# Cached keys turned in 32 by 32 blocks on VectorE instead of 128 by 128 on TensorE, in a two-layer decoder step

## The reference, cut to what matters

```python
kbar = mean(kb, axis=2)                       # kb: heads, blocks of 256 keys, 128
g = einsum('hqd,hnd->hqn', qf, kbar)          # block score; top 3 past blocks are kept
s = einsum('hqd,hqnkd->hqnk', qf, ks) - slopes * dist
p = softmax(s)                                # over the kept blocks and the own one
out = einsum('hqnk,hqnkd->hqd', p, vs)
```

## Time and profile before

| | us |
|---|---|
| median of three executions | 1229.66 |
| profiled execution, its own time | 1224.0 |
| its span | 1222.3 |
| K stage: from the own-token scores (334.3) to the last score group's end (487.1) | 152.8 |
| V stage: from there to about 638 | 151 |

### The profile page before, as it was taken

The page is one execution under the profiler, slowest core; times in us unless marked ns, Lnnn a source line. Parts: engine busy times, 40 slices in busy tenths (PEclk is TensorE's granted clock), DMA queues, the critical chain, the costliest instruction groups (busy, mean ns, idle before and its releaser), DMA issues.

```text
span 1222.3 us, 23737 instructions
## 1 busy us (share of the span) xinstructions
PE 1176.9 (96%) x9352; PEld 1042.2 (85%) x9352; DVE 713.0 (58%) x1355; ACT 564.2 (46%) x714; POOL 331.5 (27%) x207
## 2 busy tenths in 40 slices
PE   5899999999999999999999999899999989999997
PEld 2589798878888787787788898899999889999997
DVE  3746555545544546633545447489999996583112
ACT  3333324333354444422333237576666656575443
POOL 1000000000000002200000002667666778605773
PEclk9999999999999999999999999999999999999998
DMA  9999899999898878899999997585848445454542
GB/s 332 339 331 343 283 334 314 375 354 355 290 313 305 277 259 295 258 371 328 338 372 342 321 331 200 174 280 165 283 156 275 138 142 184 140 174 156 166 145 94
DMA packets 236962, 324.87 MB, mean 266 GB/s; under 512 B 12429, under 2 KB 152525, under 8 KB 236429
## 3 DMA queue, kind: packets, MB, share of 16 engines
q1 hardware_dynamic: 233472, 312.78, 75.7%
q0 software_dynamic: 2192, 7.79, 2.2%
q10 hardware_dynamic: 1188, 2.79, 0.7%
HBM read 317.96 MB, written 7.06 MB: 266 GB/s over the span
## 4 chain that ended last, share of the span: by engine, by line
PE 76%; DVE 16%; DMA 3%; issue 2%; ACT 2%; SPq 1%; POOL 0%; DVEq 0%; ACTq 0%
PE PS L307 19%; PE PS L311 18%; PE PS L310 18%; DVE PS L1763 10%; PE PS L395 5%; PE PS L987 4%; DMA XR<-in_ada_w 3%; PE PS L1014 3%; PE PS L1245 2%; DVE WLO L301 1%; PE PS L410 1%; SPq L382 1%; PE PS L1971 1%; ACT WHI L296 1%; DVE PS L1757 0%
## 5 line engine op out<-in xcount | busy, mean ns | idle before, releaser
L307 PE MATMUL PS<-HH,WHI 128*128 128x288 f32 x2176 | 662.4, 304 | 16.7 <-DVE HL L1683 4.5
L311 PE MATMUL PS<-HH,WLO 128*128 128x288 f32 x2176 | 643.9, 296 | 0.0
L310 PE MATMUL PS<-HL,WHI 128*128 128x288 f32 x2176 | 643.7, 296 | 0.0
L307 PEld LDWEIGHTS PS<-HH,WHI 128*128 128x128 f32 x2176 | 410.9, 189 | 38.2 <-issue 32.0
L296 ACT ACTIVATE WHI<-WRAW 128x1024 fp32r<-128x1024 f32 x272 | 283.8, 1056 | 344.1 <-PE PS L311 291.2
L310 PEld LDWEIGHTS PS<-HL,WHI 128*128 128x128 f32 x2176 | 411.2, 189 | 0.0
L311 PEld LDWEIGHTS PS<-HH,WLO 128*128 128x128 f32 x2176 | 410.6, 189 | 0.0
L301 POOL TENSOR_TENSOR WLO<-WRAW,WHI 128x1024 fp32r<-128x1024 f32 x117 | 281.1, 2422 | 192.6 <-ACT WHI L296 192.6
L301 DVE TENSOR_TENSOR WLO<-WRAW,WHI 128x1024 fp32r<-128x1024 f32 x155 | 191.1, 1235 | 158.1 <-ACT WHI L296 157.9
L1763 DVE SCALAR_TENSOR_TENSOR PS<-ACTS,CWT,PS 128x288 f32<-128x288 f32 x448 | 192.5, 516 | 0.0
L1739 ACT ACTIVATE ACTS<-ACTS 128x1088 f32<-128x1088 f32 x32 | 70.4, 2200 | 59.8 <-DVE ACTS L1761 34.6
(11 more groups left out here) (280 smaller groups left out, 748.1 us busy)
## 6 DMA issues: line engine op xcount, KB each, us to landing
XR<-in_ada_w SPq DMA_DIRECT2D x192, 512.0 KB, 8.5
WRAW<-in_ab_w_in SPq DMA_DIRECT2D x112, 512.0 KB, 7.3
WRAW<-in_c_w_in SPq DMA_DIRECT2D x96, 512.0 KB, 3.6
XR<-in_cache_b_k SPq DMA_DIRECT2D x128, 256.0 KB, 5.2
XR<-in_cache_b_v SPq DMA_DIRECT2D x128, 256.0 KB, 5.5
WRAW<-in_ab_w_out SPq DMA_DIRECT2D x32, 512.0 KB, 8.9
WRAW<-in_c_w_out SPq DMA_DIRECT2D x32, 512.0 KB, 3.3
ACTS<-in_x_prompt ACTq DMA_DIRECT2D x2, 1024.0 KB, 11.1
```

Source lines behind the costliest of these rows:

```text
L307: first = pe.matmul(out, whi, HH[:, k, :], start=start, stop=False)
L310: pe.matmul(out, whi, HL[:, k, :], start=False, stop=False)
L311: return pe.matmul(out, wlo, HH[:, k, :], start=False, stop=stop)
```

## The change

- TensorE turns no keys. VectorE turns each slot of XR in four instructions of 128 by 512 (`k_turn`), one per head, into four tiles KT[0] to KT[3]. The instruction turns 32 by 32 blocks in place, so a key's 128 dimensions lie as four blocks of 32, with 32 tokens of each of the four token groups on the partitions.
- The queries are spread to fit (`q_spread` on TensorE, `q_fill` on ACT and VectorE, tile BD, zeroed by GpSimd): a row of the scores is now (sequence, token group, query), and each head has columns of its own. A score group (`k_scores`) is one head: 16 float32 matmuls over 64 columns instead of 8 over 256 for two heads; there are 8 per unit instead of 4. It stands half a unit behind: heads 0 to 3 in the second half of their unit, heads 4 to 7 in the first half of the next.
- A row of a query is spread over four partitions. Gates, maxima and sums are therefore folded across partitions on TensorE (`gate_sum`, `max_turn`, `max_back`, `z_sum`), the probabilities are scaled by ACT (`row_norm`), and `probs_turn` becomes, per b, 8 pieces of 16 matmuls and one of 4, 32 columns each, where 9 transposes were.
- The mean of the gating branch moves from unit 5 to unit 2, its centring to unit 3. Page numbers are read a unit ahead.

```diff
-        def k_turn(pe, u, c, g4):
-            g, hh, j2 = 16 * u + 4 * c + g4, 2 * (c // 2) + g4 // 2, g4 % 2
-            if g >= 2:
-                pe.wait_ge((kt_a, kt_d)[g % 2], g // 2)
-            for h2 in range(2):
-                for t in range(2):
-                    at = 512 * (2 * j2 + t) + P * ((2 * hh + h2) % 4)
-                    last = pe.transpose(PS[:, (M2, M3)[g % 2], (2 * h2 + t) * P:(2 * h2 + t + 1) * P],
-                                        XR[:, c, at:at + P], IDENT[:])
-            last.then_inc(kt_tr, 1)
+        def k_turn(dve, u, c):
+            half = c // 2
+            dve.wait_ge(x_rdy[c], need(17 + u, c))
+            for x in range(4):
+                if c % 2 == 0 and (u or half):
+                    dve.wait_ge(ks_head, 8 * u + 4 * half + x - 3)
+                dve.transpose(KT[x][:, 4 * (c % 2):4 * (c % 2) + 4, :],
+                              XR[:, c].rearrange("p (a n) -> p a n", a=4)[:, :, P * x:P * x + P]).then_inc(kt_tr, 1)
+            dve.wait_ge(kt_tr, 16 * u + 4 * c + 4)
+            dve.sem_inc(x_used[c], 1)
...
-        def k_scores(pe, u, hh):
-            for h2 in range(2):
-                h = 2 * hh + h2
-                for j in range(4):
-                    last = pe.matmul(PS[32 * j:32 * j + 32, M0, 0:BLOCK], QM[:, j, h, :], KT[:, hh % 2, j, h2, :],
-                                     start=h == 0, stop=h == HEADS - 1)
+        def k_scores(pe, u, h):
+            g, h2, bank = h // 2, h % 2, (M0, M2)[u % 2]
+            pe.wait_ge(kt_tr, 16 * u + 8 * (h // 4) + 4 + h % 4 + 1)
...
+            for e in range(4):
+                for j in range(4):
+                    x = (4 * e + j) * 4 + g
+                    last = pe.matmul(PS[32 * j:32 * j + 32, bank, 64 * g:64 * g + 64], BD[:, x, 16 * h2:16 * h2 + 32],
+                                     KT[h % 4][:, 2 * j:2 * j + 2, 32 * e:32 * e + 32],
+                                     start=h2 == 0 and e == 0, stop=h2 == 1 and e == 3)
...
             for u in range(8):
-                for c in range(4):
-                        k_turn(pe, u, c, g4)
-                        rest_part(pe, n, g, x_used[c] if g4 == 3 else None)
...
+                for s in range(16):
+                    rest_part(pe, 16 + 2 * u + s // 8, s % 8)
+                    if u == 0 and s < 4:
+                        q_spread(pe, 0, s)
+                    if s % 2 and u + s // 8:
+                        k_scores(pe, u if s > 8 else u - 1, s // 2 % 4 if s > 8 else 4 + s // 2)
+                    if u == 3 and 10 < s < 15:
+                        q_spread(pe, 1, s - 11)
...
+                    if u == 7 and 6 < s < 16:
+                        probs_turn(pe, 0, s - 7)
...
+            for h in range(4, HEADS):
+                k_scores(pe, 7, h)
...
             for u in range(8):
                 for c in range(4):
+                    if (u, c) == (0, 2):
+                        q_fill(dve, 0, (0, 1))
+                    if (u, c) == (4, 2):
+                        q_fill(dve, 1, (0, 1))
...
+                    if u and c == 2:
+                        scores_take(dve, u - 1)
+                    k_turn(dve, u, c)
                     if c % 2 == 0:
                         lo(dve, 67 + 2 * u + c // 2)
+                    if (u, c) == (5, 0):
+                        choose_blocks(dve, 0)
...
+            rows = IDENT[:].rearrange("p (x i q) -> p i x q", i=4, q=DS)
+            for g in range(4):
+                for i in range(4 if t < 8 else 1):
+                    dst = PS[32 * i:32 * i + 32, probs_bank(b, f), (t % 4) * P:(t % 4 + 1) * P]
+                    last = pe.matmul(dst.rearrange("p (j r) -> p j r", j=4)[:, :, 8 * g:8 * g + 8],
+                                     SROW[b][:, g, 32 * t:32 * t + 32], rows[:, i], start=True, stop=True)
```

More of the change, by code:

```diff
@@ new lines, in q_spread @@
+        def q_spread(pe, b, e):
+            if e == 0:
+                if b:
+                    pe.wait_ge(g_ln, 1)
+                else:
+                    pe.wait_ge(s_pc, HEADS)
+                    pe.wait_ge(s_pf, HEADS)
+            rhs = Q[:, :, SR0 + 16 * b:SR0 + 16 * b + 16].rearrange("p h (s i) -> p s h i", i=DS)
+            for i in range(4):
+                dst = PS[32 * i:32 * i + 32, M3, P * e:P * e + P].rearrange("p (s h i) -> p s h i", s=4, h=HEADS)
+                last = pe.matmul(dst, IDENT[:, 32 * e:32 * e + 32], rhs, start=True, stop=True)
+            last.then_inc(s_qr, 1)
@@ new lines, in q_fill @@
+        def q_fill(eng, b, tokens):
+            eng.wait_ge(s_qr, 4 * b + 4)
+            if b:
+                eng.wait_ge(ks_head, 32)
+            else:
+                eng.wait_ge(s_bdz, 1)
+            for i in tokens:
+                src = PS[32 * i:32 * i + 32, M3, :].rearrange("p (x h q) -> p x h q", h=2, q=DS)
+                for h2 in range(2):
+                    at = 32 * h2 + DS * i
+                    dst = BD[32 * i:32 * i + 32, :, at:at + DS]
+                    if tokens[0]:
+                        eng.activation(dst, src[:, :, h2, :], ACT.Copy).then_inc(s_bdf, 1)
+                    else:
+                        eng.tensor_copy(dst, src[:, :, h2, :]).then_inc(s_bdf, 1)
@@ L1016, in k_scores, with gate_sum @@
             last.then_inc(ks_head, 1)
-        def probs_turn(pe, b, f):
-            if f:
-                pe.wait_ge(s_ptc, 3 * b + f)
-            else:
-                pe.wait_ge(s_exp, b + 1)
-            for t in range(4 * f, min(9, 4 * f + 4)):
-                n = P if t < 8 else 32
-                last = pe.transpose(PS[0:n, M1, (t % 4) * P:(t % 4 + 1) * P], SROW[:, t * P:t * P + n], IDENT[:])
-            last.then_inc(s_ptt, 1)
+        def gate_sum(pe, b):
+            pe.wait_ge(ks_free, 4 * b + 4)
+            if b:
+                pe.wait_ge(s_ptc, 3)
+            pe.matmul(PS[:, M1, 0:16], SAME, GATE.rearrange("p h n -> p (h n)"), start=True, stop=True).then_inc(s_gs, 1)
@@ new lines, in max_turn, with max_back, z_sum, probs_bank @@
+        def max_turn(pe, b):
+            pe.wait_ge(s_rm, b + 1)
+            pe.transpose(PS[0:4, M1, 0:P], RMAX, IDENT[:]).then_inc(s_mt, 1)
+        def max_back(pe, b):
+            pe.wait_ge(s_mf, b + 1)
+            pe.transpose(PS[:, M1, 128:132], MROW, IDENT[0:4, 0:4]).then_inc(s_mb, 1)
+        def z_sum(pe, b):
+            pe.wait_ge(s_exp, 4 * b + 4)
+            pe.matmul(PS[:, M1, 0:4], SAME, ZSUM, start=True, stop=True).then_inc(s_zs, 1)
+        def probs_bank(b, f):
+            return M1 if f != 1 else (M3, M0)[b]
@@ L1110, in k_act @@
             for u in range(8):
-                for c in range(4):
-                    k_save(act, u, c, 0)
-                    if c % 2 == 0:
-                        hi(act, 67 + 2 * u + c // 2)
-                    k_save(act, u, c, 2)
-                    if u < 2 and c % 2:
-                        x = 2 * u + c // 2
+                if u == 0:
+                    q_fill(act, 0, (2, 3))
+                hi(act, 67 + 2 * u)
+                if u < 2:
+                    for x in (2 * u, 2 * u + 1):
@@ new lines, in k_act, with key_bias @@
+                if u in (2, 4, 6):
+                    silu_zt(act, 51 + u // 2, u // 2 - 1)
+                if u == 6:
+                    root(act, 2)
+                if u == 7:
+                    row_norm(act, 0)
+                hi(act, 68 + 2 * u)
+                if u == 6:
+                    row_exp(act, 0)
+            for f in range(3):
+                probs_save(act, 0, f)
+        def key_bias(dve):
+            dve.wait_ge(s_iota, 1)
+            for g in range(4):
+                dve.tensor_scalar(ALB[:, g, :], IOTA, TOKROW, SLOPE[:, g:g + 1], ALU.add, ALU.mult)
@@ L2135, in _ @@
                         load_ada(sp, 32, 16, c)
+                if half and v < 7:
+                    regs = page_numbers(sp, v + 1)
                 w_load(sp, 89 + 2 * k)
```

397 lines of the change are left out of this document (216 added, 181 removed).

## The result

The changed kernel takes 1264.2 us in the median (1262.5 to 1276.3, 4 runs) where the kernel before takes 1227.2: a ratio of 1.031, 95% interval 1.027 to 1.036. It is **slower**, by 37 us. I had forecast slower by 14.6, and the time is just outside the range.

The account below looks back on a forecast made before the run. TensorE's list of instructions was taken as the bound; K stage 9.3, V stage 5.1 and 0.2 more us sum to 14.6, giving 1244 us against the median, with an 8-in-10 range of 1217 to 1264.

Parts of the forecast that it names:

- loop wait: K stage: TensorE waits 1.9 us per half unit for VectorE's turn, low part and next turn, covered by two products.
- 3.2 on top of the wait: K stage, `q_fill` for b = 1: the next score group needs three more turns and four copies, 3.2 us extra.
- 2.1: K stage: `choose_blocks`, eleven small instructions on VectorE, adds 2.1 us to the irregular part.
- TensorE waits 1.9 us in every half unit. It is then 6.5 + 1.9 = 8.45 us: K stage: a half unit takes 8.45 us instead of 8.98, so of 39 us only 8.5 remain gained.
- My list without the clock: K stage: irregular items of 26.9 us plus sixteen halves, 135.2, gave 162 us instead of 152.8.
- The V stage: 5.1 forecast: V stage: b = 1 probabilities 5.2 us instead of 1.2, and folds 1.1, on a TensorE without gaps.
- rival 5: Short matmuls bound by their issue: a score group costs 1.2 us, 23 us more, 1267 us; chance 0.10.
- Dearer turns (4): Turns of two passes, 1.14 us each: VectorE binds, K stage 203 us, whole 1285 us; chance 0.07.
- cheaper groups (2): Switches between kinds cost nothing, a score group is 0.65 us, K stage 151, whole 1232 us; chance 0.12.
- No loop wait: Turns so fast that TensorE never stands; loads at 374 GB/s bind, half a unit 7.0 us, whole 1213; chance 0.14.
- No change from SP's page numbers: SP reads page numbers while it would wait; as DMA isn't the bound, this costs nothing.
- the right mechanism: The forecast case: the loop wait takes most of what leaves TensorE; own range 1234 to 1258 us, chance 0.57.

Follow-up runs that it names:

- experiments 5: Changed kernel with the second softmax's probability pieces spread over two weight chunks of the V stage, one per two products: 1265.7 us.
- experiment 6: Changed kernel with page numbers read at the start of their unit, as before the change: 1267.9 us.
- experiment 2: Changed kernel with 16 unread matmuls on TensorE ahead of the first score group of each half unit: 1255.0 us.
- 8 to 10: Changed kernel with GpSimd low parts, spread pieces, reordered VectorE items; then three low parts ahead of GpSimd's sums of squares; then unread matmuls: 1237.5, 1229.2, 1235.7 us.
- experiment 3: Changed kernel with VectorE turning both slots of a half unit head by head, the low part ahead: 1240.9 us.
- experiment 10: Combined kernel with earlier GpSimd low parts, plus 8 to 22 unread matmuls ahead of ten score groups: 1235.7 us.
- experiment 1: Changed kernel with the low part ahead of the four turns of an even slot, not behind them: 1242.2 us.
- experiment 4: Changed kernel with the 16 low parts of the K stage on GpSimd, not on VectorE: 1249.2 us.

## Why the prediction was right or wrong

**The direction and the mechanism were right.** TensorE lost its turns and got a loop wait in exchange. The terms, forecast and measured: product 0.40 and 0.40, score group 0.83 and 0.78, turn 0.60 to the next start and 0.59 (four in 2.48, the last 0.70), loop wait 1.9 and 1.84, piece of the probabilities 0.58 and 0.58. Of the irregular waits, the first score group's was 5.58 us, that at the refill of the queries 5.45, at the block choice 3.46; "3.2 on top of the wait" and "2.1" gave 5.1 and 4.0.

**What failed is the step "TensorE waits 1.9 us in every half unit. It is then 6.5 + 1.9 = 8.45 us"**: it prices a wait by its length. The regular half that kept its clock (from 359.35; one in each of the traces of experiments 5 and 6 as well), and those of experiment 2, lasted 8.19 to 8.21; the usual half lasted 9.66 to 9.68, because the clock was at 1.2 GHz for part of the work behind the wait. That is 1.5 us, on a term of 0.53 gained per half: the sign of a regular half turned, from 8.98 before to 9.66. My list without the clock gives 161 in the table's measure, and 176.8 was measured, 15.6 more. The clock accounts for more than that: 0.85 over the 177.7 us, between the levels 1.00 and 0.50, are 53 us at 1.2 GHz, and in the half from 367.5 (0.82 over 9.70) 3.5 such us cost 1.47. At that rate 53 us cost up to 22 (an estimate, too high by the part that fell on waits). So the rest of the list came out some 5 us too high and hid part of the miss: 64 score groups at 0.78 for 0.83 are 3.2 of it, 16 waits of 1.84 for 1.9 are 1.0. The row that could have warned me was the granted clock itself: 1.00 in stages without gaps, and I took it as given for a stage into which I was putting 16 gaps of 2 us.

**The V stage: 5.1 forecast, 10.4 measured.** The pieces cost what I said. Missing were the 2.24 us stop in the middle of a piece and the low clock behind it, which together are some 3.7 of the missing 5.3 us (2.24, and the 1.47 that such a stretch cost in the regular half: an estimate); the rest stays open. Without a stop or with short ones the V stage took 152.3 to 154.3 (experiments 5, 8 to 10), 5.5 to 7.5 above before. The stop is part of rival 5 (short matmuls bound by their issue), but as a stop after a dense stretch, not as a dearer record. The floor of about 25 ns from start to start that the Trainium skill, TensorE: Matmul & The Clock Gate, gives (section on 56 ns and 53.3 ns) didn't show here: a piece's 16 matmuls (32 records) and their loads ran in 0.46 us, and the trace has them starting 17 ns apart on the mean, in four column groups side by side.

**Rivals.** Dearer turns (4) and cheaper groups (2) are excluded by the rows above. "No loop wait" (3) was tried in experiment 3: with the regular waits removed the K stage was still 155 us, not 16 halves of 7.0, and loads aren't shown as its bound, with one wait for a page of 4.4 us. In the changed kernel itself no turn waited for a page. The rates were 249 GB/s there and at most 305 (experiment 10), never the 374 that the rival assumed. "No change from SP's page numbers" held (experiment 6).

**The chances.** 0.57 for the right mechanism was fair, but the time lies above that case's own range too (1234 to 1258). The range failed because its bounds moved only the sizes of instructions; no bound was set on what a wait does to the work behind it.

## What to carry to other kernels

Work moved off the bound engine comes back if it forms a loop with it: look for the instruction that waits for the bound engine, what stands behind it in its own queue, and how much work the bound engine has to cover that round trip; one low part moved ahead of four turns was worth 22 us here. Where TensorE's list is the bound, price a new regular wait on it by more than its length: here 1.84 us cost 3.3, and 0.7 us cost 0.7. Filler that keeps the clock up pays only while it is covered by the wait (experiment 2 against 10). When engines are relieved one after the other, the next bound is near: loop, then VectorE's odd items, then pages queued behind a weight load, and the sum came out level with the kernel before.

## What the runs showed of the hardware that I had not expected

- A wait of TensorE of 0.70 us each 7.1 us left the granted clock at 1.00. Waits of 1.84 us each 9.7 us lowered it to 0.82 over the half, with steps of 0.24 instead of 0.13 us; but one of the same length in each of four traces (at 359.35 here) did not. Length alone doesn't decide: in experiment 1 the clock fell behind a wait of 1.75 us (at 466.3) and not behind one of 1.95 (at 397.2).
- After four pieces of 32 records of 32 columns at one piece each 0.98 us, TensorE stopped for 2.24 us in the fifth with no wait on another engine; at one piece each 1.38 us it did not. Seven traces have the stop (0.84 to 2.89 us), the four with spread pieces 0.60 us at most.
- VectorE instructions between SBUF tiles that began beside a 2.34 us low part on GpSimd ended only at its end or behind it (0.17 us became 1.89, 0.69 became 2.61, in experiment 4); float32 turns beside one kept their 0.67 to 0.72.
- A float32 turn of 128 by 512 in 32 by 32 blocks costs VectorE 0.59 us, as much as a two-operand instruction of the same size.
